# A chunked SSM scan with block matmuls, another order of the mixing blocks, and other first DMAs

## What is computed

```python
h = rmsnorm(x, norm1_g[l]) * (1.0 + sc1) + sh1
proj = h @ w_in[l]
q, k, v, ca, cb, su, gates = split(proj)
y_attn = sliding_window_attention(rope(q), rope(k), v, attn_sinks[l]) @ w_attn_o[l]
y_conv = conformer_conv(ca, cb, ...)            # 31 taps per channel, layernorm, silu, conv_pw_w
y_ssm = s5_ssm(su, ...)                         # below
gate_a, gate_c, gate_s = split(sigmoid(gates))
mixed = gate_a * y_attn + gate_c * y_conv + gate_s * y_ssm
x = x + g1 * (mixed @ w_out[l])
h2 = rmsnorm(x, norm2_g[l]) * (1.0 + sc2) + sh2
f_gate, f_up = split(h2 @ w_ffn_in[l])
x = x + g2 * ((silu(f_gate) * f_up) @ w_ffn_out[l])

# s5_ssm: 32 groups of 16 channels, 64 complex states each
state[t] = abar * state[t - 1] + bbar @ u[t]     # abar, bbar from a, b and log_dt
y[t] = real(c @ state[t]) + d_skip * u[t]
y_ssm = (y @ w_glu_a) * sigmoid(y @ w_glu_b)
```

## Time and profile before

| | us |
|---|---|
| median of 3 runs | 1120.54 (1117.72 to 1121.59) |
| the profiled execution | 1122.39 |
| its span in the trace | 1120.6 |
| start, until the first block of layer 0 | 60.4 |
| token mixing of layer 0 (33 blocks) | 327.8 |
| channel mixing of layer 0 (33 blocks, with the preparation of layer 1) | 222.8 |
| token mixing of layer 1 | 307.3 |
| channel mixing of layer 1, end | 202.3 |

### The profile page before, as it was taken

The page is one execution under the profiler, slowest core; times in us unless marked ns, Lnnn a source line. Parts: engine busy times, 40 slices in busy tenths (PEclk is TensorE's granted clock), DMA queues, the critical chain, the costliest instruction groups (busy, mean ns, idle before and its releaser), DMA issues.

```text
span 1120.6 us, 17763 instructions
## 1 busy us (share of the span) xinstructions
PE 982.4 (88%) x7606; PEld 890.2 (79%) x7606; DVE 755.8 (67%) x1098; ACT 463.9 (41%) x504; POOL 0.2 (0%) x4
## 2 busy tenths in 40 slices
PE   0787888878988899999998988888899879999998
PEld 0476667767878789999898977777788879999998
DVE  0479889998955546355555898999895545444444
ACT  0554555334234353345564335523423344343333
...
GB/s 327 201 113 76 189 114 173 200 184 125 193 224 235 124 145 247 254 252 225 226 263 172 166 148 83 165 129 162 115 144 234 139 113 151 188 188 188 179 123 39
DMA packets 144543, 193.78 MB, mean 173 GB/s; under 512 B 30610, under 2 KB 123666, under 8 KB 138320
## 3 DMA queue, kind: packets, MB, share of 16 engines
...
...
HBM read 191.57 MB, written 1.05 MB: 172 GB/s over the span
## 4 chain that ended last, share of the span: by engine, by line
PE 59%; DVE 27%; issue 6%; ACT 4%; ACTq 3%; DMA 0%; DVEq 0%
PE bank L451 17%; PE bank L452 16%; PE bank L453 16%; DVE yc L1327 7%; DVE wlo L1106 6%; PE bank L487 3%; ACTq L367 2%; PE bank L513 2%; PE bank L550 1%; DVE m L1291 1%; DVE prod L1303 1%; ACT whi L837 1%; DVE m L1292 1%; DVE m L1299 1%; DVE m L1294 1%
## 5 line engine op out<-in xcount | busy, mean ns | idle before, releaser
L451 PE MATMUL bank<-hhi,whi 128*128 128x256 f32 x1504 | 446.1, 297 | 23.0 <-DVE wlo L1106 14.8
L1106 DVE TENSOR_TENSOR wlo<-raw,whi 128x2048 fp32r<-128x2048 f32 x132 | 302.3, 2290 | 231.7 <-PE bank L453 173.0
L452 PE MATMUL bank<-hlo,whi 128*128 128x256 f32 x1504 | 436.3, 290 | 0.0
L453 PE MATMUL bank<-hhi,wlo 128*128 128x256 f32 x1504 | 435.8, 290 | 0.0
L451 PEld LDWEIGHTS bank<-hhi,whi 128*128 128x128 f32 x1504 | 300.1, 200 | 52.5 <-issue 34.9
L837 ACT ACTIVATE whi<-raw 128x2048 fp32r<-128x2048 f32 x132 | 251.7, 1908 | 159.5 <-DMA raw<-in_w_in 53.0
L452 PEld LDWEIGHTS bank<-hlo,whi 128*128 128x128 f32 x1504 | 300.0, 199 | 0.2
L453 PEld LDWEIGHTS bank<-hhi,wlo 128*128 128x128 f32 x1504 | 299.5, 199 | 0.0
L451 PE MATMUL bank<-bhi,whi 128*128 128x256 f32 x608 | 176.4, 290 | 18.8 <-DVE wlo L1106 4.3
L452 PE MATMUL bank<-blo,whi 128*128 128x256 f32 x608 | 174.0, 286 | 0.0
L453 PE MATMUL bank<-bhi,wlo 128*128 128x256 f32 x608 | 173.9, 286 | 0.0
...
## 6 DMA issues: line engine op xcount, KB each, us to landing
...
```

Source lines behind the costliest of these rows:

```text
L451: mm(o, w_hi, a_hi, start=start, stop=False, skip_group_check=True)
L452: mm(o, w_hi, a_lo, start=False, stop=False, skip_group_check=True)
L453: return mm(o, w_lo, a_hi, start=False, stop=stop, skip_group_check=True)
L1106: V.tensor_tensor(wlo[mi % N_LO][:, :], raw[SLOT[("main", *divmod(mi, NB))]][:, :], whi[mi % N_HI][:, :].bitcast(F32), ALU.subtract).then_ ...
```

## The change

- The 256 tokens are taken as 64 chunks of 4 steps. `ssm_in` now sums the 4 steps of a chunk in PSUM, with B times the powers of abar as weights: 128 float32 matmuls of 64 columns, with 32 rows of weights each, over four banks. `ssm` scans 64 chunks instead of 256 tokens, in two halves of 8 tiles. `ssm_out` applies C times powers of abar to the states of the chunks: 64 matmuls of 63 columns for each half. `ssm_within` adds what happens inside a chunk: 16 matmuls with the block-diagonal weights `kf`.
- The weights for that are prepared on the chip: `b_source` (B times powers), ten `prep_round`s of four transpositions instead of four, `c_powers` (C times powers), and `taps_round` (64 small matmuls for `kf`). In layer 0 this stands between blocks 1 and 6, for layer 1 in the channel mixing of layer 0. The table of cos and sin is one quarter of the size.
- The order of the blocks is su, su, q, q, kv, cb, ca, cb, ca, gs x4, the four SSM output blocks, ga x4, ao x2, gc x4, cp x2, wo x4. The branches are now summed in the order SSM, attention, convolution, so the block ahead of `wo` is `cp`.
- c has a DMA of its own, the first on SP, and a transposition of its own; x is next after the first w_mod block on SP; the small vectors are issued by ACT; constants, B and C by POOL. The `EARLY` tiles are gone: all w_mod blocks go through the ring of four. `norm_root(0)` and `spread(0)` stand ahead of the modulation's columns.

```diff
-    names = [("su", 0), ("q", 0), ("q", 1), ("kv", 0), ("cb", 0), ("ca", 0), ("cb", 1), ("ca", 1)]
-    names += [("ga", n) for n in range(4)] + [("su", 1), ("ao", 0), ("ao", 1)]
+    names = [("su", 0), ("su", 1), ("q", 0), ("q", 1), ("kv", 0), ("cb", 0), ("ca", 0), ("cb", 1), ("ca", 1)]
+    names += [("gs", n) for n in range(4)] + [("glb", 0), ("gla", 0), ("glb", 1), ("gla", 1)]
+    names += [("ga", n) for n in range(4)] + [("ao", 0), ("ao", 1)]
     names += [("gc", n) for n in range(4)] + [("cp", 0), ("cp", 1)]
-    names += [("gs", n) for n in range(4)] + [("glb", 0), ("gla", 0), ("glb", 1), ("gla", 1)]
     names += [("wo", n) for n in range(4)]
...
-SSM_PAIRS = [3, 7, 11, 15, 34, 38, 42, 45]
-SSM_IN_AT = {t: n for n, t in enumerate(SSM_PAIRS)}
-SSM_OUT_AT = {t + 4: n for n, t in enumerate(SSM_PAIRS)}
-SSM_AT = {t + 2 * c: 2 * n + c for n, t in enumerate(SSM_PAIRS) for c in range(2)}
-SSM_Y_AT = {SSM_PAIRS[4 * n + 3] + 4: n for n in range(2)}
-SSM_SPLIT_AT = SSM_PAIRS[7] + 4
-ROPE_Q_AT, ROPE_K_AT = 8, 9
+Z_AT = (12, 6)
+SSM_AT = [{z + 1: 0, z + 4: 1} for z in Z_AT]
+SSM_OUT_AT = [{z + 5: 0, z + 9: 1} for z in Z_AT]
+SSM_Y_AT = [z + 10 for z in Z_AT]
+SSM_SPLIT_AT = [z + 11 for z in Z_AT]
+ROPE_Q_AT, ROPE_K_AT = 17, 18
...
-SCORES_AT = {11 + 4 * r: r for r in range(4)}
+SCORES_AT = {19 + 3 * r: r for r in range(4)}
...
-CONV_AT = {18 + n: divmod(n, 8) for n in range(16)}
-CONV_MEAN_AT, CONV_VAR_AT = 35, 36
+ATT_SPLIT_AT = 2 * AT[("ga", 0)] + 1
+UC_PAD_AT = 11
+CONV_AT = {20 + 3 * n // 2: divmod(n, 8) for n in range(16)}
+CONV_MEAN_AT, CONV_VAR_AT = 46, 48
...
+B_AT = [{}, {PREP_AT + 2: (0,), PREP_AT + 3: (1,)}]
+C_AT = [1, PREP_AT + 5]
+ROUND_AT = [{2 + n: (2 * n, 2 * n + 1) for n in range(ROUNDS // 2)}, {2 * (PREP_AT + 4 + n) + 1: (n,) for n in range(ROUNDS)}]
+TABLE_AT = [4, 2 * (PREP_AT + 10)]
+POWERS_AT = [[7, 9], [2 * (PREP_AT + 15), 2 * (PREP_AT + 17)]]
+TAPS_AT = [11, 2 * (PREP_AT + 19)]
+DECAY_AT = [12, 2 * (PREP_AT + 20)]
...
-EARLY = [("mod", 0, 0, k) for k in range(N_RAW, DK)]
-MOD_ITEMS = ITEMS[:N_RAW] + EARLY + [x for x in ITEMS[N_RAW:] if x[0] == "mod"]
...
-            for n, item in enumerate(ITEMS[:N_RAW] + EARLY[:-1] + ITEMS[N_RAW:N_RAW + 1] + EARLY[-1:] + ITEMS[N_RAW + 1:]):
-                if n == 1:
-                    small_vectors(sp, 0)
+            for item in ITEMS:
+                if item == ITEMS[1]:
+                    load_x(sp)
...
+            def ssm_in(l):
+                pe.wait_ge(u_ready, 2 * l + 2)
+                pe.wait_ge(bc_cp, ROUNDS * (l + 1))
+                if l == 0:
+                    pe.wait_ge(kf_ready, 1)
+                for k in range(CT):
+                    for a in range(2):
+                        for j in range(STEPS):
+                            for q in range(4):
+                                r = slice(32 * q, 32 * q + 32)
+                                o = b_z[q][:, (2 * k + a) * NC:(2 * k + a + 1) * NC]
+                                last = mm(o, bl[r, a, STEPS - 1 - j, k, :], u_ssm[r, k, j * NC:(j + 1) * NC],
+                                          start=(k == 0 and a == 0 and j == 0), stop=(j == STEPS - 1), skip_group_check=True)
+                last.then_inc(z_ready, 1)
...
+            def ssm_within(l):
+                pe.wait_ge(kf_ready, l + 1)
+                pe.wait_ge(z_used, 2 * l + 1)
+                for k in range(CT):
+                    o = b_out[k // 2][:, (k % 2) * T:(k % 2 + 1) * T]
+                    for t in range(STEPS):
+                        mm(o[:, t * NC:T], kf[:, k, t, :], u_ssm[:, k, 0:(STEPS - t) * NC], start=(k % 2 == 0 and t == 0), stop=False, skip_group_check=True)
...
+            def ssm_out(l, half):
+                pe.wait_ge(s_ready, 2 * l + half + 1)
+                s = state[half].rearrange("p a (q c n) -> p a q c n", q=2, c=CT)
+                for k in range(CT):
+                    for j in range(STEPS):
+                        c0 = (k % 2) * T + j * NC
+                        for a in range(2):
+                            for q in range(2):
+                                r = 32 * (2 * half + q)
+                                last = mm(b_out[k // 2][r:r + 32, c0 + 1:c0 + NC], ca[:, a, j, 4 * k + 2 * half + q, :], s[:, a, q, k, 0:NC - 1],
+                                          start=False, stop=(a == 1), skip_group_check=True)
+                last.then_inc(y_ready, 1)
...
+                            mm(o[r:r + 32, k * P:k * P + 32], bk[:, a, s, :], ct[:, a, s, :],
+                               start=(k == 0 and a == 0), stop=False, skip_group_check=True)
+                            last = mm(o[r:r + 32, k * P + 32:(k + 1) * P], bk[:, a, s, :], ca[:, a, 0:STEPS - 1, s, :],
+                                      start=False, stop=(a == 1), skip_group_check=True)
...
+            late_constants(pool)
+            b_and_c(pool, 0)
...
-            load_x(act)
-            late_constants(act)
-            b_and_c(act, 0)
-            act.wait_ge(vec_cp, 1)
-            fn(cact[:, :], vec[0][:, R_C:R_C + DK], ACT.Silu).then_inc(silu_c, 1)
...
+            small_vectors(act, 0)
+            act.wait_ge(c_tr, 1)
+            fn(cact[:, :], b_mod[:, 0:DK], ACT.Silu).then_inc(silu_c, 1)
...
+                step(tt(x0, inputs(a), factor(0), ALU.mult))
+                then(tt(x1, inputs(1 - a), factor(1), ALU.mult))
+                then(tt(x0, x0, x1, (ALU.subtract, ALU.add)[a]))
+                for g in range(2):
+                    last = V.tensor_scalar(bsrc[a][:, :, g * GROUP:(g + 1) * GROUP], bt[0].rearrange("p (x i) -> p x i", i=GROUP),
+                                           consts[:, 8 + g:9 + g], None, ALU.mult)
+                last.then_inc(bc_src, 1)
...
+                step(tt(ca[:, a], outputs(a), power(0), ALU.mult))
+                then(tt(spare, outputs(1 - a), power(1), ALU.mult))
+                last = tt(ca[:, a], ca[:, a], spare, (ALU.add, ALU.subtract)[a])
...
+            def ssm(l, half):
+                if half == 0:
+                    dve.wait_ge(tab_ready, l + 1)
+                    dve.wait_ge(z_ready, l + 1)
+                else:
+                    dve.wait_ge(s_ready, 2 * l + 1)
...
+                    step(tt(by_cos[:, q], z, cs, ALU.mult))
+                    last = tt(by_sin[:, q], z, sn, ALU.mult)
+                    if q == 0:
+                        step(last)
+                last.then_inc(z_used, 1)
+                dve.wait_ge(z_used, 2 * l + half + 1)
+                step(tt(s5[:, 0], by_cos[:, :, :, 0], by_sin[:, :, :, 1], ALU.add))
+                step(tt(s5[:, 1], by_cos[:, :, :, 1], by_sin[:, :, :, 0], ALU.subtract))
+                r = decay[:, 2 * half:2 * half + 2].rearrange("p q c n -> p (q c n)")
+                for a in range(2):
+                    dve.wait_ge(s_dve, step.n - 1)
+                    step(V.tensor_tensor_scan(s[:, a], r, s[:, a], 0.0, ALU.mult, ALU.add))
+                cs, sn = (b.rearrange("p q c n -> p (q c n)").rearrange("p (o x) -> p o x", o=1).to_broadcast([P, 2, 512]) for b in tabs)
+                c2, s2 = (b.rearrange("p (a x) -> p a x", a=2) for b in turned)
+                dve.wait_ge(s_dve, step.n)
+                step(tt(c2, s, cs, ALU.mult))
+                then(tt(s2, s, sn, ALU.mult))
+                step(tt(s[:, 0], c2[:, 0], s2[:, 1], ALU.subtract))
+                tt(s[:, 1], s2[:, 0], c2[:, 1], ALU.add).then_inc(s_ready, 1)
...
             lo(0)
+            norm_root(0)
```

598 lines of the change are left out of this document (332 added, 266 removed).

## The result

The change takes the median from 1120.17 us (4 runs) to 1087.49 us (1083.96 to 1090.81, 4 runs), a ratio of 0.9712 with a 95% interval of 0.9687 to 0.9737. The prediction was 1101, with 1068 to 1124 as the range: the sign and the range hold, and the gain is 33 us where 20 were forecast.

A forecast was written before the change was run, and what follows sets the result against it. PE was taken to bound channel mixing, PE with waits partly for DVE token mixing, and a chain behind ACT's queue the start. Terms −14 + 0 + 10 − 16 = −20 took 1122.4 to 1102.4, as a median 1101; range 1068 to 1124.

The forecast's parts named there:

- PE's work: Token mixing: PE busy 299 us in layer 0 (278.5 before) and 276 in layer 1 (266.1 before).
- DVE: Token mixing: DVE's busy time falls from 269.3 to about 234 us in layer 0, from 253.2 to 199 in layer 1.
- The price of `ssm_in`: SSM on PE, each layer: 256 records at 0.11 us each, 28.2 us.
- The bound that I had from L587: `ssm_in` on PE: at 0.06 us a record, as in L587's alternating row halves, it could take 15.4 us.
- rival B: Row groups hide each other's loads: `ssm_in` takes 15.4 us instead of 28.2; total 1075, range 1060 to 1085; chance 0.24.
- The other small matmuls: PE: `ssm_within` 4.3 us and `ssm_out` 10.2 in each layer; `taps_round` +5.1 in each preparation.
- The idle time of PE: Token mixing: PE's idle time falls from 49.3 to 28 us in layer 0, from 41.2 to 15 in layer 1.
- The start: Before block 0: it begins at 46 us instead of 60.4, a term of −14 (bounds −23 and 0).
- my 8.4: Start: 8.4 us between the end of the last w_mod block's matmuls and block 0, taken from the earlier profile.
- The allowance of 5.5 us: Start: 46 taken over 40.5, because eight w_mod blocks share four tiles and the last four loads wait.
- The channel mixing of layer 0: Preparation for layer 1: rounds 3.6, `taps_round` 5.1 and 1.3 for DVE's long pieces, +10 us on a busy PE.
- The waits early in layer 0: Layer 0's mixing: about 20 us of PE idle early, waiting for the preparation chain ahead of `lo` of blocks 5 and 6.

## Why the prediction was right, and where its terms were wrong

The mechanism was right in its main part: DVE's SSM held up PE in token mixing, and the channel mixing pays for the added preparation. ACT's queue held the start, but was worth 3.5 us of it. That the total came within 14 us is luck in part: PE's work was put 45 us too high, and the waits, the start and the channel mixing together 31 too low. With PE's work as measured and the rest as forecast, the sum would have been 1056, outside the range. Point by point:

- **DVE** was sized well: 232.5 and 200.1 us, forecast 234 and 199; a half of the SSM is 9.7 us (from 125.78 to the `lo` at 135.49), forecast 10.
- **The price of `ssm_in`** is the term that failed by most: "I take 28.2, because the L495 row is the one with full-width weights". It was 7.4. L495 has all 128 rows in each load, so that no group can work beside another. The bound that I had from L587, 0.06, has two groups in turn, and it was met: two groups gave 0.056. That row should have been read by its row groups, with four groups half of it. The rival B had the mechanism, at 15.4 us and a chance of 0.24, and underrated it too. By its share of the sum the term is 21 us in each layer, 42 in all.
- **The other small matmuls**: `ssm_out` 7.4 for 10.2 and `taps_round` 2.0 for 5.1 were too dear, `ssm_within` 4.9 for 4.3 a little too cheap.
- **The idle time of PE** went the other way: "The idle 49.3 becomes 28" was 38.2, and "the idle 41.2 falls to 15" was 25.7. The run with less DVE work in the kernel before shows why: with 41 us taken away, 32.9 and 28.2 remained. The SSM on DVE was a third of PE's idle time and not the two fifths to two thirds that these terms take away. What the forecast had no term for is that the new order puts the reads of `gla`'s results behind the convolution on DVE, 7.9 and 11.1 us of PE's waits. PE's work was forecast 45 us too high in the two stages, its waiting 21 too low, the start 8 too early and the channel mixing 3 too short: the sum came out 14 too high.
- **The start**: 46 forecast, 53.6 measured. From the last w_mod block to block 0 it is 6.6 us (46.96 to 53.58), less than my 8.4. What I left out stands ahead of that: the last two w_mod blocks come behind the sums of squares, a wait of 4.5 us and 6.96 at the lower clock, so that they end at 46.96 and not at 32. The allowance of 5.5 us that I made was for their loads, and PE takes both without a wait for one. With the squares first block 0 came at 48.9.
- **The channel mixing of layer 0**: +12.2 for +10, of which PE's work is 7.1 (forecast 8.7) and its waiting 5.1 (forecast 1.3).
- **The waits early in layer 0** (about 20 forecast) are there: 3.7, 5.8, 0.9 and 2.5 are the ones in the first six blocks, 13 us. The 6.9 us pieces of `c_powers`, which I held for a part of them, cost 0.9 where they stand; half a block later PE waited 5.3 us for them.

How far the gain comes from the new order of the blocks was not tried by itself. With the old SSM on DVE that order would ask for all 16 tiles, 74 us by the earlier trace rows, in the blocks ahead of `glb`, so it is bound to the shorter scan. How the 33 us divide between the two is open.
